# Reordering the mixing stage of a hybrid transformer block: modulation in quadrants, decay tiles on two engines, another order of attention steps

## The chip, the cores and the metric

The program runs on one core of one Trainium2 chip. The metric is the device time of one execution in microseconds. Lower is better. Engines are named as in the profile: PE is TensorE, PEld its weight loads, DVE VectorE, ACT ScalarE, POOL GpSimd, and SP the engine that issues most DMAs. All data is float32.

## What is computed

A first block of the model (512 tokens, width 1024) with four mixers and a mixture of experts, then two layers of a second block. The part that matters here is the first block up to its output projection:

```python
mod = silu(c) @ ada_w + ada_b
sh1, sc1, g1, sh2, sc2, g2 = split(mod, 6)
h = rms_norm(x, norm1_g) * (1 + sc1) + sh1
y = hybrid_mixer(h)
x = x + g1 * y
h = rms_norm(x, norm2_g) * (1 + sc2) + sh2

# hybrid_mixer: proj = h @ w_in, split in columns for
# a: differential attention, 4 heads of 2 maps, keys of 32
# b: block attention (block 256, top 3: all causal keys here), 4 heads of 64
# c: gated linear attention, chunks with decay:
bcum = cumsum(g)
o_inter = (q * exp(bcum)) @ state
att = einsum(q_i, k_j, exp(bcum_i - bcum_j)), causal
o = o_inter + att @ v
state = exp(b_last) * state + (k * exp(b_last - bcum)).T @ v
# d: gated linear recurrence (conv of 4, sigmoid gates, scan, gelu)
```

## The kernel before

The program is a row of stages, each a block in which every engine has its own instruction list. The lists meet at a barrier at the end of each block, and semaphores order them within. The stages concerned are, in order: `project1_stage` (h @ w_in), `mixing_stage`, `attention_stage` under the name "mix", a transpose stage "turn_mix" and the output projection "out1". After them come the second norm, the routing, the experts and the second block.

Weights flow through a ring of three slots of 2 MB, filled by SP in the order of the plan (`load_chunks`). A chunk is loaded into its slot once the matmul group that read the slot's last chunk is done. The mixing stage uses eight chunks of ada_w, and the chunks of w_out follow.

`mixing_stage` does four things at once. Its order is written out by hand, one list per engine.
- **Modulation.** `modulate(i)` on PE multiplies the condition vector, spread over the columns of `cond_rows`, by chunk i of ada_w, so that the result stands in all rows it fills: 512 columns as two halves of 64 rows and 256 columns, for eight blocks of the contraction, and a matmul with `ones` for the bias. `take_mod(i)` on ACT copies each half to both halves of the rows of `k.mod`. That row is used by later stages. There are two banks for it, so `modulate(i)` waits for `take_mod(i - 2)`.
- **Gated linear attention (c).** DVE sums the decays to `b`. For each tile t of 128 tokens, the tensor `ksub[:, t]` holds, for each of 8 reference positions, the keys with their relative decay. It is made in three steps: POOL subtracts the reference and clamps (L1048, 8 instructions of 128x128 a tile, the decay spread), ACT takes the exponential (`raise_tile`), DVE multiplies by the keys (`key_tile`). The queries `qsub` are made by DVE, per head into its own 32 rows (L1403), from the exponential of `ex` (ACT, L1246). Then, for each tile: `att_tile` (PE, 8 matmuls), `mask` (DVE), `outputs` and `update` (PE), `next_state`, `take_out` and `sum_out` (DVE).
- **Gated recurrence (d).** `convolve` (DVE), `lru_gates` (PE), sigmoids and exponentials (ACT), a product `gated` (DVE, L1392) and `lru_tail` (DVE).
- **Head norms of a and b.** `square` (ACT, with `ksub[2]` and `ksub[3]` as room for the squares, which is why the decay spread of tile 2 waits for all four sums), `sum_squares` and `normalize` (DVE), `turn` (PE transposes of q and k into banks) and `take_turned` (ACT for even numbers, DVE for odd ones).

`attention_stage` runs 24 steps. A step is a pair of maps for one tile i of 128 queries: scores against 128(i + 1) keys (L634), transposes of the exponentials (L647), and values (L658). The list of PE is software-pipelined:

```python
for n in range(n_steps):
    if n + 2 < n_steps:
        scores(n + 2)
    if n + 1 < n_steps:
        turn(n + 1)
    values(n)
```

Each pass of that loop is called a round here. Sixteen steps are of differential attention, whose two maps use 32 rows of PE each. Eight are of block attention, with 64 rows each. They stand one kind after the other; within a head i runs 3, 2, 1, 0 or 0, 1, 2, 3. Beside them, `HeadNorm` does one product on the modulation row (DVE, round 0), and the norm of the finished differential heads (square at round 16, sum at 17, root at 22, product at 23).

## Time and profile before

| what | value |
|---|---|
| median of 3 runs | 3010.74 us (3009.67 to 3011.48) |
| the profiled execution's own time | 3006.7 us |
| its span in the trace | 3004.9 us |
| its mean granted clock of PE | 0.952 |
| mixing stage | about 213.6 to 289.6 us |
| attention stage "mix" | about 289.6 to 371.5 us |
| busy over the whole span | PE 92%, DVE 39%, ACT 26%, POOL 11% |

A row of a timeline gives the start in microseconds from the span's start, how long the row lasted, the engine, the line, the operation, what it writes and reads, shapes, how many instructions are merged in it (x) and, in brackets, for how long its engine was idle before it and what ended the wait.
### The profile page before, as it was taken

The page shows a single profiled execution, that of the slowest core. Times are in us where ns is not written, and L with a number is a line of the kernel's source. Part 1 is how long each engine was busy: PE and PEld are TensorE (multiplying, and loading weights), DVE is VectorE, ACT ScalarE, POOL GpSimd, SP SyncE. Part 2 cuts the span into 40 slices and gives each one's busy share as a digit, 9 for nine tenths or more (in the row PEclk, how much of TensorE's full clock was granted, in tenths as well). Part 3 has the DMA queues.
Part 4 walks back from the last instruction along what each step waited for, and adds up shares of the span by engine and source line. Part 5 has one row for each costly group of instructions (what it writes and reads, how often), then busy time and mean ns, then how long its engine had stood idle before and what let it go on. Part 6 is the DMA issues. An engine that isn't in the chain of part 4 may idle for free. (4 is left out here: it accounts for less than half of the span.)

```text
span 3004.9 us, 55460 instructions
## 1 busy us (share of the span) xinstructions
PE 2776.7 (92%) x21321; PEld 1848.2 (62%) x21322; DVE 1180.6 (39%) x2449; ACT 789.6 (26%) x1689; POOL 316.7 (11%) x415
## 2 busy tenths in 40 slices
PE   5998977989998989999978999999999999899997
PEld 4986774333333323333337677788887768788886
DVE  1235644222222222232224575434343566454332
ACT  3225520000000000010104355322232345343221
POOL 1003000222222212222220000000000000000000
PEclk8998886999999989999999999999999999999999
DMA  7244027999999999799964400122232220023220
GB/s 200 78 138 172 1 78 295 401 409 398 402 407 411 399 411 408 292 399 407 409 251 130 139 1 2 56 91 106 84 112 61 83 85 2 30 83 111 85 104 37
DMA packets 181479, 583.68 MB, mean 194 GB/s; under 512 B 31243, under 2 KB 70348, under 8 KB 132108
## 3 DMA queue, kind: packets, MB, share of 16 engines
q1 hardware_dynamic: 160422, 557.17, 47.4%
...
## 5 line engine op out<-in xcount | busy, mean ns | idle before, releaser
L1846 PE MATMUL moe_up<-expert_w,mod 128*32 128x512 f32 x2040 | 244.9, 611 | 28.7 <-issue 19.5
L1957 DVE TENSOR_TENSOR mod<-moe_up,mod 128x512 f32<-128x512 f32 x85 | 58.8, 692 | 480.2 <-PE moe_up L1846 479.2
L1846 PE MATMUL moe_up<-ring,mod 128*32 128x512 f32 x1696 | 209.3, 619 | 22.2 <-DMA ring<-in_exp_w_up 17.3
L303 PE MATMUL mlp_bank<-mlp_hT_hi,mlp_w 128*128 128x512 f32 x512 | 199.7, 390 | 0.0
L304 PE MATMUL mlp_bank<-mlp_hT_lo,mlp_w 128*128 128x512 f32 x512 | 199.5, 390 | 0.0
L305 PE MATMUL mlp_bank<-mlp_hT_hi,mlp_w 128*128 128x512 f32 x512 | 199.5, 390 | 0.0
L304 PE MATMUL mlp_bank<-mlp_w,mlp_u_hi 128*128 128x512 f32 x512 | 199.5, 390 | 0.0
L305 PE MATMUL mlp_bank<-mlp_w,mlp_u_lo 128*128 128x512 f32 x512 | 199.5, 390 | 0.0
L303 PE MATMUL mlp_bank<-mlp_w,mlp_u_hi 128*128 128x512 f32 x512 | 199.5, 390 | 0.0
L1934 ACT ACTIVATE mod<-mod 128x256 f32<-128x256 f32 x85 | 35.4, 417 | 565.7 <-DVE mod L1959 565.7
L347 ACT ACTIVATE mlp_w<-ring 128x1024 fp32r<-128x1024 f32 x128 | 125.1, 1052 | 207.6 <-PE mlp_bank L305 207.6
L1846 PEld LDWEIGHTS moe_up<-expert_w,mod 128*32 128x32 f32 x2040 | 63.2, 112 | 170.5 <-issue 141.0
L356 DVE TENSOR_TENSOR mlp_w<-ring,mlp_w 128x1024 fp32r<-128x1024 f32 x128 | 148.1, 1220 | 6.1 <-ACT mlp_w L347 6.1
L1808 POOL DMA_INDIRECT mixed_rows<-mod,moe_place x86 | 135.8, 1579 | 122.0 <-DVE mod L1974 113.6
L1846 PEld LDWEIGHTS moe_up<-ring,mod 128*32 128x32 f32 x1696 | 51.0, 112 | 136.4 <-issue 91.9
L1863 PE MATMUL moe_down<-expert_w,mod 128*32 128x256 f32 x2176 | 133.0, 381 | 0.0
L1462 DVE TENSOR_TENSOR x<-x,mlp_bank 128x512 f32<-128x512 f32 x64 | 43.9, 687 | 222.2 <-PE mlp_bank L305 222.2
L1930 ACT ACTIVATE mod<-moe_turn_hid 128x256 f32<-128x256 f32 x85 | 32.6, 383 | 341.1 <-PE moe_turn_hid L1854 341.1
L2524 DVE TENSOR_TENSOR mlp_relu<-mlp_relu 128x512 f32<-128x512 f32 x64 | 44.3, 692 | 191.5 <-ACT mlp_u_hi L2521 191.5
L1797 POOL CAST moe_index<-row_token 128x1 uint32 (+1 forms) x87 | 20.1, 232 | 857.3 <-PE moe_turn_rows L1839 613.8
L303 PEld LDWEIGHTS mlp_bank<-mlp_hT_hi,mlp_w 128*128 128x128 f32 x512 | 96.2, 188 | 20.5 <-DVE mlp_hT_lo L510 0.4
L305 PEld LDWEIGHTS mlp_bank<-mlp_w,mlp_u_lo 128*128 128x128 f32 x512 | 96.2, 188 | 20.0
...
## 6 DMA issues: line engine op xcount, KB each, us to landing
...
```

Source lines behind the costliest of these rows:

```text
L303: nc.tensor.matmul(out, lhsT.hi, rhs.hi, start=(i == 0), stop=False)
L304: nc.tensor.matmul(out, lhsT.hi, rhs.lo, start=False, stop=False)
L305: mm = nc.tensor.matmul(out, lhsT.lo, rhs.hi, start=False, stop=last)
L347: nc.scalar.activation(halves.hi[:, at], w[:, at], ACT.Copy).then_inc(hi_made, 1)
L356: nc.vector.tensor_tensor(halves.lo[:, at], w[:, at], halves.hi[:, at].bitcast(F32), ALU.subtract).then_inc(lo_made, 1)
L1462: return nc.vector.tensor_tensor(k.x[:, t, cols], k.x[:, t, cols], psum, ALU.add)
L1808: pool.indirect_dma_start(x_parts, bass.IndirectOffsetOnAxis(ap=place[:], axis=0), y, None, compute_op=op).then_inc(y_stored, 16)
L1846: mm = nc.tensor.matmul(up[quarter[q], :], rowsT[:, c % 2, quarter[c // 2]], w[:, q], start=(c == 0), stop=(c == UPS - 1))
L1863: mm = nc.tensor.matmul(down[quarter[q], 0:YCOLS], hidT[:, h, quarter[at]], w[:, h, q * YCOLS:(q + 1) * YCOLS], start=(at == 0 and h == 0) ...
L1934: nc.scalar.activation(sig, gate, ACT.Sigmoid, scale=ALPHA).then_inc(sig_ready, 1)
L1957: nc.vector.tensor_tensor(pre, up[:], bias_up, ALU.add).then_inc(up_taken, 1)
L2524: chain(nc.vector.tensor_tensor(r, r, r, ALU.mult))
```

## The change

In `mixing_stage`:
- A modulation is computed in four quadrants of 32 rows and 128 columns each. ACT copies it with one instruction into `mod_rows`. In the attention stage SP stores four rows of that tile to DRAM and reads them back with one DMA into all rows of `k.mod`; the load of `norm2_row` moves there too.
- The decay spread of tiles 0 and 2 is on DVE, as two instructions of 128x1024 each; tiles 1 and 3 stay on POOL. The queries are one product on DVE and four copies on POOL. The product `gated` goes from DVE to POOL, as two instructions.
- The lists of PE, ACT and DVE are in another order, and two of the turned copies go from DVE to ACT.

In the attention stage the two kinds of steps alternate (two differential ones, one of the others) for the first 15 steps, and the work beside them is at other rounds: the product on the modulation row at round 19, the head norm at rounds 21 to 23.

```diff
+class MixRest:
...
+    def sync(self, sp):
+        sp.dma_start(self.norm2_row[:], row(self.k.a["norm2_g"][0])).then_inc(self.norm2_loaded, 16)
+        sp.dma_start(self.mod_dram.rearrange("(i q n) -> q i n", q=PARTS, n=COL // PARTS), self.mod_rows[0:P:BR]).then_inc(self.rows_stored, 16)
+        sp.wait_ge(self.rows_stored, 16)
+        sp.dma_start(self.k.mod[:].rearrange("p i n -> p (i n)"), row(self.mod_dram)).then_inc(self.rows_spread, 16)
+        sp.wait_ge(self.rows_spread, 16)
 
     def scalar(self, act, n):
         nc = self.k.nc
         if n == self.made:
             act.wait_ge(self.out_taken, self.made)
             nc.scalar.activation(self.sq[:], self.v, ACT.Square).then_inc(self.squared, 1)
-        if n == self.n_steps - 2:
+        if n == self.made + 1:
             act.wait_ge(self.summed, 1)
             nc.scalar.activation(self.rms[:], self.ss[:], ACT.Sqrt, bias=self.k.eps[:], scale=1.0 / A_DV).then_inc(self.rooted, 1)
 
     def vector(self, dve, n):
         k, nc = self.k, self.k.nc
-        if n == 0:
-            dve.wait_ge(k.norm2_loaded, 16)
+        if n == self.made - 2:
+            dve.wait_ge(self.norm2_loaded, 16)
+            dve.wait_ge(self.rows_spread, 16)
             nc.vector.scalar_tensor_tensor(k.mod[:, 2, :], k.mod[:, 2, :], 1.0, self.norm2_row[:], ALU.add, ALU.mult)
         if n == self.made + 1:
             dve.wait_ge(self.squared, 1)
             nc.vector.tensor_reduce(self.ss[:], self.sq[:], X, ALU.add).then_inc(self.summed, 1)
-        if n == self.n_steps - 1:
+        if n == self.made + 2:
             dve.wait_ge(self.rooted, 1)
             nc.vector.reciprocal(self.inv[:], self.rms[:]).then_inc(self.inverted, 1)
...
-            nc.gpsimd.tensor_copy(cond_rows[:], k.cond[:].unsqueeze(2).to_broadcast([P, ND, half])).then_inc(spread, 1)
-            nc.gpsimd.memset(qsub[:], 0.0).then_inc(zeroed, 1)
-            for t in range(NT):
-                pool.wait_ge(cum, t + 1)
-                if t == 2:
-
-                    pool.wait_ge(summed, len(heads))
+            def spread_tile(t):
                 bt = b[:, tile(t)]
                 for n in range(NSUB):
                     ref = bt[:, n * SUB + SUB // 2:n * SUB + SUB // 2 + 1]
-                    nc.gpsimd.tensor_scalar(ksub[:, t, n, :], bt, ref, -DECAY_CLAMP * C_TAU, ALU.subtract, ALU.max).then_inc(key_spread, 1)
+                    nc.gpsimd.tensor_scalar(ksub[:, t, n, :], bt, ref, -DECAY_CLAMP * C_TAU, ALU.subtract, ALU.max).then_inc(key_spread[1], 1)
+
+            nc.gpsimd.tensor_copy(cond_rows[:], k.cond[:].unsqueeze(2).to_broadcast([P, ND, BR])).then_inc(spread, 1)
+            nc.gpsimd.memset(qsub[:], 0.0).then_inc(zeroed, 1)
+            pool.wait_ge(cum, 2)
+            spread_tile(1)
+            pool.wait_ge(q_scaled, 1)
+            pool.wait_ge(zeroed, 1)
+
+            pool.wait_ge(key_spread[1], NSUB)
+            for h in range(C_HEADS):
+                r = slice(h * C_DK, (h + 1) * C_DK)
+                nc.gpsimd.tensor_copy(qsub[r, :, h, :], ex[r, :].rearrange("p (n s) -> p n s", s=SUB)).then_inc(qsub_made, 1)
+            pool.wait_ge(opened, 4)
+            pool.wait_ge(conv_done, 2)
+            pool.wait_ge(qsub_made, C_HEADS)
+            for j in range(2):
+                nc.gpsimd.tensor_tensor(xc[:, j, :], xc[:, j, :], gates[:, 1, j, :], ALU.mult).then_inc(gated, 1)
+            pool.wait_ge(cum, NT)
+
+            pool.wait_ge(summed, len(heads))
+            spread_tile(3)
...
-                    for h in range(2):
-                        nc.tensor.matmul(to[half * h:half * h + half, 0:width], cond_rows[:, j, :], w[:, j, width * h:width * h + width],
+                    for q in range(PARTS):
+                        nc.tensor.matmul(to[BR * q:BR * q + BR, 0:width], cond_rows[:, j, :], w[:, j, width * q:width * q + width],
                                          start=(j == 0), stop=False)
-                for h in range(2):
-                    mm = nc.tensor.matmul(to[half * h:half * h + half, 0:width], k.ones[0:1, 0:half],
-                                          k.mod[0:1, part, c + width * h:c + width * (h + 1)], start=False, stop=True)
+                for q in range(PARTS):
+                    mm = nc.tensor.matmul(to[BR * q:BR * q + BR, 0:width], k.ones[0:1, 0:BR],
+                                          k.mod[0:1, part, c + width * q:c + width * (q + 1)], start=False, stop=True)
                 mm.then_inc(k.groups_done, 1)
...
-            modulate(2)
-            modulate(3)
+            for i in range(2, 6):
+                modulate(i)
...
             def take_mod(i):
-                n = chunks[i]
-                part, c = (n - FIRST_MOD) * COL // D, n * COL % D
                 act.wait_ge(k.groups_done, first_group + i + 1)
-                for h in range(2):
-                    src = mod_bank[i % 2][half * h:half * h + half, 0:width]
-                    for to in range(2):
-                        copy = nc.scalar.activation(k.mod[half * to:half * to + half, part, c + width * h:c + width * (h + 1)], src, ACT.Copy)
-                copy.then_inc(mod_taken, 1)
+                nc.scalar.activation(mod_rows[:, i, :], mod_bank[i % 2][:, 0:width], ACT.Copy).then_inc(mod_taken, 1)
...
-            nc.scalar.activation(silu, silu, ACT.Silu).then_inc(silu_made, 1)
-            nc.scalar.activation(dxg[:, 2:4, :], dxg[:, 2:4, :], ACT.Gelu_apprx_tanh).then_inc(gelu_made, 1)
...
+            nc.scalar.activation(silu, silu, ACT.Silu).then_inc(silu_made, 1)
             square_out(0)
+            nc.scalar.activation(dxg[:, 2:4, :], dxg[:, 2:4, :], ACT.Gelu_apprx_tanh).then_inc(gelu_made, 1)
...
+            def spread_tile(t):
+                bt = b[:, tile(t)]
+                ref = bt.rearrange("p (n s) -> p n s", s=SUB)[:, :, SUB // 2:SUB // 2 + 1].to_broadcast([P, NSUB, P])
+                chain(nc.vector.tensor_tensor(ksub[:, t], bt.unsqueeze(1).to_broadcast([P, NSUB, P]), ref, ALU.subtract))
+                nc.vector.tensor_scalar(ksub[:, t], ksub[:, t], -DECAY_CLAMP * C_TAU, None, ALU.max).then_inc(key_spread[0], 1)
...
+            spread_tile(0)
...
+            nc.vector.tensor_tensor(ex[:], fm[:, 0, :], ex[:], ALU.mult).then_inc(q_scaled, 1)
...
-            nc.vector.tensor_tensor(xc[:], xc[:], gates[:, 1], ALU.mult).then_inc(gated, 1)
...
-            for h in range(C_HEADS):
-                r = slice(h * C_DK, (h + 1) * C_DK)
-                nc.vector.tensor_tensor(qsub[r, :, h, :], fm[r, 0, :].rearrange("p (n s) -> p n s", s=SUB),
-                                        ex[r, :].rearrange("p (n s) -> p n s", s=SUB), ALU.mult).then_inc(qsub_made, 1)
...
-            take_turned(1)
-            sum_out(3)
             take_turned(3)
...
-            take_turned(5)
             take_turned(7)
...
-            attention_stage(k, "mix", [diff_step(h, i) for h in range(A_HEADS) for i in tiles(h)]
-                            + [moba_step(g, i) for g in range(2) for i in tiles(g)], beside=lambda ctx, sems: HeadNorm(k, tok, norm2_row, ctx, *sems))
+            diffs = [diff_step(h, i) for h in range(A_HEADS) for i in tiles(h)]
+            mobas = [moba_step(g, i) for g in range(2) for i in tiles(g)]
+            steps = []
+            for n in range(5):
+                steps += [diffs[2 * n], mobas[n], diffs[2 * n + 1]]
+            steps += diffs[10:] + mobas[5:]
+            attention_stage(k, "mix", steps, beside=lambda ctx, out_taken: MixRest(k, tok, mod_rows, mod_dram, ctx, out_taken, 5 * 3 + 6))
```

What the table of orders looks like at three places. First ACT, from the end of its logarithms to the exponential of `ex` and the queries' and keys' decays behind it (`mod<-mixing_bank` and `mod_rows<-mixing_bank` are the modulation's copies, `mixing_ksub<-tok` the squares of the head norm, `mixing_ksub<-mixing_ksub` a decay tile). Before:

```order
L1203 ACTIVATE mixing_ksub<-tok 128x1024 x2
L1196 ACTIVATE mod<-mixing_bank 64x256 x4
L1238 ACT_TABLE_LOAD
L1238 ACTIVATE qk<-mixing_bank,lru_b 128x512 x2
L1203 ACTIVATE mixing_ksub<-tok 128x1024
L1238 ACTIVATE qk<-mixing_bank,lru_b 128x512 x2
L1203 ACTIVATE mixing_ksub<-tok 128x1024
L1196 ACTIVATE mod<-mixing_bank 64x256 x4
L1243 ACTIVATE qk<-qk 128x512 x2
L1196 ACTIVATE mod<-mixing_bank 64x256 x4
L1246 ACT_TABLE_LOAD
L1246 ACTIVATE mixing_ex<-mixing_ex 128x512
```

and with the change:

```order
L1213 ACTIVATE mod_rows<-mixing_bank 128x128
L1219 ACTIVATE mixing_ksub<-tok 128x1024 x2
L1253 ACT_TABLE_LOAD
L1253 ACTIVATE qk<-mixing_bank,lru_b 128x512 x2
L1213 ACTIVATE mod_rows<-mixing_bank 128x128
L1253 ACTIVATE qk<-mixing_bank,lru_b 128x512 x2
L1213 ACTIVATE mod_rows<-mixing_bank 128x128
L1257 ACTIVATE qk<-qk 128x512 x2
L1259 ACT_TABLE_LOAD
L1259 ACTIVATE mixing_ex<-mixing_ex 128x512
```

Two squares have left this stretch and stand behind the exponential, and each modulation's copy is one instruction. The silu and gelu activations, which opened the list, are gone from ahead of it.

Second PE, from the modulation ahead of the first attention tile to the second tile of the gated linear attention (L1098, later L1124, is the turn of the keys). Before:

```order
L1062 MATMUL mixing_bank<-ring,mixing_cond_rows 64x256 x16
L1065 MATMUL mixing_bank<-mod,ones 64x256 x2
L1098 MATMUL mixing_bank<-ident,mixing_kout 128x128
L1088 MATMUL mixing_bank<-mixing_qsub,mixing_ksub 128x64 x8
L1062 MATMUL mixing_bank<-ring,mixing_cond_rows 64x256 x16
L1065 MATMUL mixing_bank<-mod,ones 64x256 x2
L1088 MATMUL mixing_bank<-mixing_qsub,mixing_ksub 128x64 x8
```

and with the change:

```order
L1088 MATMUL mixing_bank<-ring,mixing_cond_rows 32x128 x32
L1091 MATMUL mixing_bank<-mod,ones 32x128 x4
L1124 MATMUL mixing_bank<-ident,mixing_kout 128x128
L1114 MATMUL mixing_bank<-mixing_qsub,mixing_ksub 128x64 x8
L1088 MATMUL mixing_bank<-ring,mixing_cond_rows 32x128 x32
L1091 MATMUL mixing_bank<-mod,ones 32x128 x4
L1114 MATMUL mixing_bank<-mixing_qsub,mixing_ksub 128x64 x8
```

Ahead of the first of these rows stand five modulations where there were three. One follows between the tiles as before, and one stands ahead of the last tile; before, one stood there, one ahead of the last outputs and one among the turns.

Third POOL, its whole list in the mixing stage. Before:

```order
L1038 COPY mixing_cond_rows<-cond 128x512
L1039 MEMSET mixing_qsub 128x2048
L1048 ISA
L1048 TENSOR_SCALAR mixing_ksub<-mixing_b 128x128 x32
```

and with the change:

```order
L1055 COPY mixing_cond_rows<-cond 128x256
L1056 MEMSET mixing_qsub 128x2048
L1053 ISA
L1053 TENSOR_SCALAR mixing_ksub<-mixing_b 128x128 x8
L1065 COPY mixing_qsub<-mixing_ex 32x32x16 x4
L1070 TENSOR_TENSOR qk<-qk 128x512 x2
L1053 TENSOR_SCALAR mixing_ksub<-mixing_b 128x128 x8
```

POOL spreads two tiles instead of four, and between them it places the queries and does the product for the recurrence.

## Rows read from the trace of the kernel before

**Rows 1.** windows: us, PE, PEld, DVE, ACT, POOL busy; PEclk; DMA share, GB/s

```profile
213.60:289.60 76.00, 66.78 (x491) 45.11 (x491) 50.78 (x82) 46.95 (x86) 30.38 (x34) 0.84 0.61 214
289.60:371.50 81.90, 78.52 (x504) 61.27 (x504) 49.50 (x132) 40.26 (x124) 0.00 (x0) 0.79 0.01 2
291.50:325.60 34.10, 33.62 (x148) 25.49 (x145) 17.39 (x44) 13.53 (x44) 0.00 (x0) 0.50 0.00 1
240.00:245.00 5.00, 1.42 (x7) 1.42 (x8) 4.91 (x7) 4.96 (x12) 5.00 (x5) 0.53 1.04 385
```

**Rows 2.** timeline of ACT, mixing stage: start, length, instruction, [idle before]

```profile
213.70 1.28 ACT L1221 ACT_TABLE_LOAD   x1 [0.27 <-PEq L256]
...
217.37 1.06 ACT L1222 ACTIVATE dxg<-dxg 128x1024 f32<-128x1024 f32 x1
...
235.02 1.55 ACT L1196 ACTIVATE mod<-mixing_bank 64x256 f32<-64x256 f32 x4
...
237.88 0.63 ACT L1246 ACTIVATE mixing_ex<-mixing_ex 128x512 f32<-128x512 f32 x1
```

**Rows 3.** timeline of DVE, mixing stage

```profile
229.01 0.54 DVE L1387 TENSOR_SCALAR qk<-qk,mixing_lru_lam 128x512 f32<-128x512 f32 x1
...
232.76 1.21 DVE L1392 TENSOR_TENSOR qk<-qk 128x1024 f32<-128x1024 f32 x1
...
238.60 3.01 DVE L1403 TENSOR_TENSOR mixing_qsub<-fm,mixing_ex 32x512 f32<-32x512 f32 x4 [3.24 <-ACT mixing_ex L1246]
...
275.04 0.68 DVE L1314 TENSOR_TENSOR mixing_att<-mixing_bank,upper_incl 128x512 f32<-128x512 f32 x1
...
287.94 1.40 DVE L1357 TENSOR_SCALAR qk<-mixing_bank,gain_cols 128x512 f32<-128x512 f32 x2
```

**Rows 4.** groups of POOL: instruction, count | busy us, mean ns | idle before

```profile
L1048 POOL TENSOR_SCALAR mixing_ksub<-mixing_b 128x128 f32<-128x128 f32 x32 | 28.0, 891 | 8.6 <-DVE mixing_b L1374 8.6
...
L2067 POOL TENSOR_TENSOR tok<-tok,cos_a 128x512 f32<-128x512 f32 x2 | 4.3, 2156 | 0.2
...
L1038 POOL COPY mixing_cond_rows<-cond 128x512 f32<-128x512 f32 x1 | 0.6, 610 | 201.4 <-POOLq L256 201.4
```

**Rows 5.** timeline of PE, mixing stage

```profile
243.58 0.48 PE L1098 MATMUL mixing_bank<-ident,mixing_kout 128*128 128x128 f32 x1 [5.36 <-DVE mixing_kout L1407]
243.85 3.52 PE L1088 MATMUL mixing_bank<-mixing_qsub,mixing_ksub 128*128 128x64 f32 x16
...
270.34 2.00 PE L1088 MATMUL mixing_bank<-mixing_qsub,mixing_ksub 128*128 128x64 f32 x16
...
273.60 0.32 PE L1131 MATMUL mixing_bank<-tok,mixing_kt 128*32 128x64 f32 x8
273.85 3.67 PE L1062 MATMUL mixing_bank<-ring,mixing_cond_rows 128*64 128x256 f32 x32
```

**Rows 6.** page, part 5: a group of the expert stage

```profile
L1863 PE MATMUL moe_down<-expert_w,mod 128*32 128x256 f32 x2176 | 133.0, 381 | 0.0
```

**Rows 7.** timeline of PE, attention stage

```profile
289.90 1.13 PE L634 MATMUL mix_s<-qk 32*128 32x512 f32 x4 [1.83 <-PEq L974]
...
295.27 1.22 PE L634 MATMUL mix_s<-qk 32*128 32x256 f32 x4
...
322.35 1.92 PE L647 MATMUL mix_t<-ident,mix_p 128*128 128x128 f32 x8
...
326.18 0.92 PE L634 MATMUL mix_s<-qk 32*128 32x384 f32 x4
...
329.86 0.70 PE L634 MATMUL mix_s<-qk 32*128 32x256 f32 x4
...
346.92 0.92 PE L634 MATMUL mix_s<-qk 64*128 64x384 f32 x4
```

**Rows 8.** timeline of PE in norm_rows_stage, later in the program

```profile
440.63 1.58 PE L577 MATMUL norm_bank<-ident,h 128*128 128x128 f32 x8 [0.36 <-DVE h L556]
```

**Rows 9.** window of that place, columns as in rows 1

```profile
441.00:443.00 2.00, 1.24 (x9) 1.01 (x7) 2.00 (x3) 0.00 (x0) 0.00 (x0) 0.83 0.68 264
```

133 lines of the change are left out of this document (69 added, 64 removed).

## The prediction

> **What bounds the kernel now.** I read the windows first. The change touches two stages that run one after the other behind barriers: mixing_stage, 213.6 to 289.6 us, and the attention stage, 289.6 to 371.5 us [rows 1]. What comes later (expert stage, second block) starts when they end, so a microsecond saved here is one saved at the end. In the mixing stage PE is busy 66.8 of 76.0 us, yet no single engine is the bound: the chain of waits moves between them. The timelines show it. ACT is busy without a gap from 213.7 to the exponential at 237.88 [rows 2]; DVE makes the masked queries from it, 238.60 to 241.6 [rows 3]; PE has waited 5.36 us when it goes on at 243.58 [rows 5], now at 1.2 GHz. Then PE is the path, its modulation among the attention tiles, up to 275; from the last mask at 275.04 DVE works without a gap to 289.34 [rows 3]. In the attention stage PE is busy 78.5 of 81.9 us [rows 1], and 34.1 us of it lie at PEclk 0.50, the lower of its two levels.
>
> **The mixing stage, part by part.**
> *ACT's opening.* The silu and gelu activations leave the front: 213.70 to 218.43 with two table loads, 4.7 us [rows 2]. They come back behind the last decay tile with the same two loads. Three modulation copies stand ahead of the exponential; each was four instructions in 1.55 us [rows 2] and becomes one of 128x128. By the rate of those, 0.38 us for 256 columns, I take 0.28, so 3.8 us less. Two squares of 1.05 us go behind it. That is 10.6 us of work less, but ACT now runs into waits (gate matmul 1.2 us, third modulation 1.5 us, others 1.1): the exponential ends near 231.7, not 238.51. DVE, which adds one spread tile here (a subtraction of 1.21 us and a clamp of twice 0.54 [rows 3], 2.4 us in all), is ready by then.
> *Queries.* DVE's four products take 3.01 us [rows 3]. Now one product (0.7) and four POOL copies follow. The trace has no 32x512 POOL copy: the nearest is 0.61 us for 128x512, the far bound is a POOL product of 2.16 us [rows 4]. I take 0.61: queries ready at 235.1, at worst 241.3.
> *PE up to the first tile.* Modulations 0 to 5 now all stand ahead of it. One costs 3.67 us plus 0.58 for the bias at full clock [rows 5]. In quadrants it is 72 matmuls of 128 columns instead of 36 of 256. The short quadrant matmuls of 64 columns start 31 ns apart (eight in the 0.25 us from 273.60 to 273.85 [rows 5]); those of 256 columns in the expert stage 61 ns apart (133.0 us over 2176 [rows 6]). 128 columns lie between; I take 33 ns, as the columns add little to the first: 2.4 us each, 3.9 us at 1.2 GHz. The weights limit it now: 2.1 MB at 385 GB/s [rows 1] are 5.4 us a chunk, and a slot frees when its modulation ends (the first three near 219, 223.5 and 228). The third chunk is in near 220, the next three follow near 226, 231 and 237. So modulation 5 starts at 236.8, the clock having fallen in the gap before it, and ends at 240.8; the first tile starts at 241.1 against 243.85. The POOL copies, even at mid-range, are hidden behind this wait.
> *PE from there to the last mask.* Before, 31.2 us (243.85 to 275.04). Now, at full clock: tile 2.0 [rows 5], modulation 2.4, tile 2.0, outputs 1.0, update and key turn 0.6, tile 2.0, outputs 1.7, update and turn 0.6, modulation 2.4, tile 2.0, outputs 1.4, update 0.3, state and hand-off 0.5: 18.9. The last mask is at 260.0. The decay tiles must keep up: tile 2 is spread by DVE by 241.8, tile 3 by POOL after its copies and two gating products of 2.16 us [rows 4], 239.4 to 246.4 at 0.89 us each for eight. ACT then raises it, runs silu, and DVE has tile 3 ready at 253.1, 2.6 us before PE asks.
> *DVE's tail.* 14.3 us before. Two of its four turned copies go to ACT (2 x 0.7 [rows 3]), one sum goes ahead, one product comes in: 13.5. The end is at 273.5 against 289.34: 15.8 us less. I take 15, as a dozen hand-offs are rounded down. Bounds: matmuls at 61 ns delay every modulation by 2.0 us and eat 8 to 9 us; a clock at 1.2 GHz through the tiles costs 3; POOL copies at 2.16 us cost up to 5, by the third decay tile. DVE or POOL faster than taken gives 2 back. So 7 to 18.
> *The DMAs.* norm2_row (0.5 MB) leaves the mixing stage's queue; in the attention stage SP issues it, a 16 KB store, waits, and a 2 MB spread. At 385 GB/s they need about 7 us plus two landings; DVE asks for them at step 19 of 24, some 45 us on. Hidden. Nothing is queued on SP behind them.
>
> **The attention stage.** The matmuls are the same, in another order. The price of the clock is in the trace: seven rounds at 1.2 GHz took 30.9 us (295.27 to 326.18), the seven of the same shapes at 2.4 GHz 17.1 us (329.86 to 346.92) [rows 7]. The question is when the clock rises. Before, it fell 1.6 us into the stage after a gap of 1.8 us, and came back only at 325.6, in a stretch that holds eight transposes and the values after them (from 322.35 [rows 7]). The opening before had a 384-column and a 256-column score step on 32 rows, with eight and six transposes. Now the second step is a 64-row one of 512 columns, its two matmuls filling all rows of the array, and eight transposes, 384 columns, and eight transposes follow. That is denser than anything in the first 30 us before. I expect the rise 5 to 8 us in, so nearly all of 13.8 us is saved. Against it: the first scores now run at 1.2 GHz, since PE stands half idle before the stage (+1.1); the product on the modulation row, 1.22 us on DVE, moves from a slack round into one where DVE has little room (+1.2). The head norm now ends in the last three rounds; its square, sum and root fit beside values still running, at most +1. Sum: 11 us less. Bounds: 13.8 less if all goes at full clock, 0 if it rises as late as before.
> Do transposes count for the clock? In norm_rows_stage PE does nothing but transposes, and the granted clock rises within them, 0.83 over 441 to 443 us [rows 8, 9]. The Trainium skill ("TensorE: Matmul & The Clock Gate", Part 4) says that full clock does not engage for transposes; by that rule the rise would hang on scores and values alone, and the sum would be 15 instead of 26. The trace disagrees with it.
>
> **Rivals.**
> 1. The clock rises late: the opening is too thin, small steps follow, and only the two long steps 11 and 12 lift it, three rounds later than before. For it: 34 us at 0.50 before [rows 1]. Mixing keeps 15, attention gives 0 to -3: 2996. The skill's rule on transposes would give this one.
> 2. The quadrant matmuls start no faster than about 61 ns apart: modulation costs 4.4 us as before, mixing gains 7, attention 11: 2993. For it, rows 6; against it, the 31 ns. The skill (same page, Part 2, step 2) names about 62 ns per matmul where the sequencer decodes in microcode; that is this rival, and the 31 ns speak against it here.
> 3. Slower: the mixed order keeps the attention stage at 1.2 GHz to its end. A round costs 2.0 us more there (13.8 over 7). The 15 of mixing are used up once the clock stays low for eight rounds beyond the seven of before; with all 23 rounds it is 16 x 2.0 - 15 = 17 slower: 3028. Against it: steps of both long kinds come early.
> 4. The change doesn't shorten mixing because POOL's work (copies, gating, third decay tile) is twice what I take; tile 3 is late by 5 to 7 us: 2990.
>
> **The numbers.** Sum: -15 and -11, 26 us. The profiled execution took 3006.7 us (span 3004.9), 4 us under the median of 3010.7; against the median the forecast is 2985, for the profile a span near 2979. Chances: both gains 0.55, rival 1 0.2, rival 2 0.1, rival 4 0.08, rival 3 0.03, several of these together 0.04. The range, from both gains at their upper ends (18 and 13) to rival 1 with a poorer mixing stage (10 and 0): 2979 to 3000. A measurement tells about 0.2%, 6 us, from no change. Faster by more 0.93, within 0.03, slower 0.04.
>
> **What would show it.** Right: exponential of ex ending near 232, first tile near 241, mixing stage about 60 us long, attention stage about 70 with PEclk 1.00 from its tenth microsecond. Wrong: modulation over 3 us at full clock; PE waiting for chunks past 240; tile 3's clamp on POOL past 248; PEclk 0.50 past 290.

## The result, and the profile after

The changed kernel took 2980.97 us (median of four runs, 2976.33 to 2988.59), the kernel before 3010.49 us beside it (four runs, 3009.67 to 3011.48). The ratio is 0.9894, with a 95% interval of 0.9858 to 0.9930; times 3010.49 that is 2978.6 us. The forecast was 2985 in a range of 2979 to 3000, so the median lies just inside the lower end and the time by the ratio 0.4 us below it; the interval is 2968 to 2989 us, far wider than that distance. Something else stands out: the kernel before spread over 1.8 us, the changed one over 12.3. The profiled execution is the slowest of its four runs (span 2986.8, own time 2988.59).

Windows of the changed kernel, columns as in [rows 1]: the mixing stage, the attention stage, and within it the stretch at the lower clock.

```profile
214.15:274.32 60.17, 48.10 (x780) 38.75 (x780) 50.66 (x80) 38.16 (x65) 25.15 (x24) 0.83 0.74 263
274.32:351.17 76.85, 73.36 (x504) 56.90 (x505) 49.12 (x132) 40.22 (x125) 0.00 (x0) 0.87 0.10 35
276.30:296.80 20.50, 20.03 (x88) 15.78 (x87) 8.17 (x17) 8.00 (x24) 0.00 (x0) 0.50 0.30 115
```

From first matmul to first matmul, mixing went from 76.2 us (213.74 to 289.90) to 60.2, attention from 81.7 (to 371.58) to 76.9. What follows took 2.3 us longer than before, beginning at once: the transposes behind attention ran at full clock before (2.81 us at 371.58) and here fall into a stretch at 1.2 GHz (4.48 us). With a start 0.4 us later the sum is -18.1, the difference of the spans. The 2.3 us are not all the change's: what follows attention took 2633.3, 2637.7 and 2636.7 us in the three profiles of the kernel before, and 2635.6, 2639.9 and 2635.6 in those of the changed one.

PE in the changed kernel: the mixing stage, for [rows 5], and the first transposes behind the attention stage:

```profile
215.96 1.95 PE L1088 MATMUL mixing_bank<-ring,mixing_cond_rows 128*32 128x128 f32 x64
...
233.43 3.64 PE L1088 MATMUL mixing_bank<-ring,mixing_cond_rows 128*32 128x128 f32 x64 [3.38 <-DMA ring<-in_ada_w]
...
238.80 3.58 PE L1088 MATMUL mixing_bank<-ring,mixing_cond_rows 128*32 128x128 f32 x64 [1.14 <-DMA ring<-in_ada_w]
...
242.83 1.90 PE L1114 MATMUL mixing_bank<-mixing_qsub,mixing_ksub 128*128 128x64 f32 x16
...
351.17 4.48 PE L403 MATMUL turn_mix_bank<-ident,tok 128*128 128x128 f32 x24 [2.12 <-PEq L596]
```

ACT, for [rows 2]: the exponential of the decay differences, and that of the fourth decay tile, which waits for POOL.

```profile
230.42 0.63 ACT L1259 ACTIVATE mixing_ex<-mixing_ex 128x512 f32<-128x512 f32 x1
...
247.77 1.06 ACT L1223 ACTIVATE mixing_ksub<-mixing_ksub 128x1024 f32<-128x1024 f32 x1 [2.63 <-POOL mixing_ksub L1053]
```

POOL (in [rows 4] it only spread tiles and the conditions): the second tile, the four query copies, the two gating products, the fourth tile.

```profile
223.94 7.73 POOL L1053 TENSOR_SCALAR mixing_ksub<-mixing_b 128x128 f32<-128x128 f32 x8 [7.65 <-DVE mixing_b L1398]
231.93 4.19 POOL L1065 COPY mixing_qsub<-mixing_ex 32x512 f32<-32x512 f32 x4 [0.26 <-DVE mixing_ex L1414]
236.30 3.48 POOL L1070 TENSOR_TENSOR qk<-qk 128x512 f32<-128x512 f32 x2 [0.18 <-POOL mixing_qsub L1065]
239.95 7.79 POOL L1053 TENSOR_SCALAR mixing_ksub<-mixing_b 128x128 f32<-128x128 f32 x8 [0.17 <-DVE mixing_ss L1318]
```

DVE, for [rows 3]: the last mask and the last turned copy.

```profile
260.20 0.68 DVE L1339 TENSOR_TENSOR mixing_att<-mixing_bank,upper_incl 128x512 f32<-128x512 f32 x1
...
273.24 0.75 DVE L1384 TENSOR_SCALAR qk<-mixing_bank,gain_cols 128x512 f32<-128x512 f32 x1 [0.40 <-PE mixing_bank L1173]
```

The four runs carry a hint about the spread. Their spans and mean granted clocks give the time at 1.2 GHz (a mean of 0.954 over 2986.8 us is 275 us at half clock): 275 us in the slowest, 244 in the fastest (2974.5, 0.959). So 31 us of lower clock go with 12.3 us of time. The clock is given to three digits, and one unit of the last is 6 us at 1.2 GHz, so this is a rough figure.

### The profile page after: what moved, and what is told of

Read it like the earlier page. It is cut to its first block and busy times, and to the rows that moved or that the text cites. A ratio compares the mean times of both kernels' runs of the same rounds, so it can differ in the third digit from the quotient of the medians.

```text
span 2986.8 us, 56010 instructions
## 1 busy us (share of the span) xinstructions
PE 2756.0 (92%) x21609; PEld 1838.9 (62%) x21610; DVE 1180.0 (40%) x2447; ACT 781.1 (26%) x1667; POOL 312.8 (10%) x405
## 5 line engine op out<-in xcount | busy, mean ns | idle before, releaser
L303 PEld LDWEIGHTS mlp_bank<-mlp_w,mlp_u_hi 128*128 128x128 f32 x512 | 96.2, 188 | 19.9
## 6 DMA issues: line engine op xcount, KB each, us to landing
expert_w<-in_exp_w_up SPq DMA_DIRECT2D x97, 1024.0 KB, 10.8
hT<-in_exp_w_up SPq DMA_DIRECT2D x24, 1024.0 KB, 10.8
```

The source lines that it names most:

```text
L303: nc.tensor.matmul(out, lhsT.hi, rhs.hi, start=(i == 0), stop=False)
```

## The experiments

There were eighteen experiments, on four chips; five of them ran a kernel that had run before, unedited. "Stage" is from first matmul to first matmul, "low" the time at 1.2 GHz within it, in each one's profile. Times of different chips are not compared where it can be helped; the experiments told in one section did not all run on the same chip. The kernel before took part each time: over these four chips it has 89 runs.

### Is it one kernel or several? The changed kernel and the one before, again

> The changed kernel again, unedited, to see whether its runs differ among themselves by the same amount and by the same cause. The four runs known so far lie 12.3 us apart (2976.33 to 2988.59) where those of the kernel before lie 1.8 us apart, and the slowest of them spent about 275 us at the lower clock (span 2986.8, mean granted clock 0.954) against 244 us in the fastest (2974.5, 0.959): 31 us of lower clock for 12.3 us of time. Theory (the clock in the attention stage rises sooner in some runs and later in others): times between 2975 and 2989, the profiled run's attention stage 66 to 75 us long, and the time of a run grows by about 0.4 us with each us at 1.2 GHz. Rival (the spread comes from DMAs or from elsewhere in the span): mean granted clock the same in every run while the times differ, attention 74.7 us again. Rival (an accident of the chip it ran on): runs within 2 us of each other.

> The kernel before once more, unedited, with a profile. On the chips used since the first comparison its runs fall into two groups, 3009 to 3015 us at a mean granted clock of 0.950 and 3027 to 3033 us at 0.944, nothing between; the profile known is of the first group. 18 us for about 44 us more at 1.2 GHz. Theory (the second group keeps 1.2 GHz through a stretch of one of its two stages, as the changed mixing stage did in one profile): if the profiled run is of the second group, its mixing stage is near 90 us instead of 76.2, or its attention stage near 98 instead of 81.7, and the rest within 3 us of the first profile. Rival (the whole span is a little slower): stages longer in proportion, by 0.6%. If the profile is of the first group again, stages within 1 us of the first profile, and nothing is told of the second.

> The kernel before, one more profile, for the group of runs at 3027 to 3033 us. The attention stage in the old order was seen at 1.2 GHz for 34 us in two profiles of the kernel before and for 72 us in a profile of the changed mixing stage with the old order, where it took 102.4 us instead of 81.1 and the clock rose only when the first 64-row steps came. Theory: if this run is of the slow group its attention stage is 98 to 103 us long at 1.2 GHz for some 70 us, mixing 76 us. Rival: mixing 90 us or more with attention 81.7. If it is of the first group it shows the first profile's stages again and nothing more.

The changed kernel again: 2983.8 us (six runs, 2982.7 to 2992.0), ratio 0.9883 (0.9850 to 0.9916). This profile caught the other way in which its attention stage goes:

```profile
213.20:273.00 59.80, 46.03 (x780) 37.41 (x780) 50.67 (x80) 38.05 (x65) 24.91 (x24) 0.89 0.75 265
273.00:341.90 68.90, 65.53 (x505) 50.43 (x506) 48.98 (x132) 40.33 (x125) 0.00 (x0) 0.98 0.10 40
274.90:278.30 3.40, 3.06 (x14) 1.70 (x10) 1.93 (x2) 2.12 (x6) 0.00 (x0) 0.50 0.60 188
```

Mixing is the same to 0.4 us. Attention is 8.0 us shorter, with 17 us less at 1.2 GHz, on the same instructions. The spread is there again (9 us, up to 2992.0, a little over the 2989 expected), so the rival of an accident falls, and the two profiles show that the clock in attention is part of it. It is not all of it. The span is only 5.0 us shorter (2981.8 against 2986.8), as what follows attention took 4.3 us longer in this profile. Over the sixteen runs of the unedited changed kernel, time grows by 0.29 us per us of lower clock, with a correlation of 0.77.

The kernel before does the same on a larger scale. Of its 89 runs 48 lie between 3007 and 3018 us (median 3011.4, the lower group) and 41 between 3025 and 3033 (3029.6, the upper group), with none between; the four of the first comparison were all of the lower group, which with 48 to 41 is an accident of four draws. Over the 23 runs on the first of these chips, time grows by 0.43 us per us of lower clock. The second profile was of the lower group and repeated the first (stages 76.0 and 81.7). The third, at 3029.4 us, was of the upper one:

```profile
214.70:291.80 77.10, 67.70 (x493) 45.68 (x493) 50.78 (x82) 46.99 (x87) 30.36 (x34) 0.85 0.61 212
291.80:390.80 99.00, 95.52 (x504) 74.95 (x504) 50.01 (x132) 40.06 (x124) 0.00 (x0) 0.64 0.00 1
293.80:365.50 71.70, 70.86 (x313) 55.65 (x312) 33.76 (x92) 25.42 (x84) 0.00 (x0) 0.50 0.00 1
```

From first matmul to first matmul attention is 99.1 us, 17.4 longer than the 81.7 of the first profile, and mixing 0.9 us; that is the group. PE was busy for 70.9 of the 71.7 us at 1.2 GHz. The clock came back in the first round with a 64-row score step (PE, same profile):

```profile
360.33 2.08 PE L634 MATMUL mix_s<-qk 64*128 64x512 f32 x4
362.34 0.39 PE L636 MATMUL mix_s<-causal_half,ident_half 128*128 128x128 bf16 x2
362.53 1.91 PE L647 MATMUL mix_t<-ident,mix_p 128*128 128x128 f32 x8
364.24 2.01 PE L658 MATMUL mix_o<-tok,mix_pt 128*128 128x64 f32 x12
366.18 0.92 PE L634 MATMUL mix_s<-qk 64*128 64x384 f32 x4
```

In the lower group it came back without any 64-row step. The first line is from the first profile of the kernel before, where the clock rose at 325.6; the second is the same round in this profile, where it did not:

```profile
320.15 2.08 PE L634 MATMUL mix_s<-qk 32*128 32x512 f32 x4
```
```profile
322.04 2.08 PE L634 MATMUL mix_s<-qk 32*128 32x512 f32 x4
```

What the two places share is that a round with 512-column scores follows another one. The scores of the first pair start at 314.94 and 320.15 in the first profile and at 316.82 and 322.04 in this one; those of the next pair, whose second step is the first with 64 rows, at 355.12 and 360.33 in this one. So the number of rows alone does not explain when the clock rises.

### The two halves of the change, each alone

The new mixing stage with the old attention order (diff), and the old mixing stage with the new order (the same lines the other way round in the kernel before, its `made` at 21):

```diff
-            steps = []
-            for n in range(5):
-                steps += [diffs[2 * n], mobas[n], diffs[2 * n + 1]]
-            steps += diffs[10:] + mobas[5:]
-            attention_stage(k, "mix", steps, beside=lambda ctx, out_taken: MixRest(k, tok, mod_rows, mod_dram, ctx, out_taken, 5 * 3 + 6))
+            steps = diffs + mobas
+            attention_stage(k, "mix", steps, beside=lambda ctx, out_taken: MixRest(k, tok, mod_rows, mod_dram, ctx, out_taken, 16))
```

> The changed kernel with the attention steps in the order of before (all sixteen differential steps, then the eight others), the squares of the head norm made at step 16: only the mixing stage and the place of the small DMAs are new. Theory (the two gains are separate, some 15.5 us in mixing and the rest in the order of the steps): 3010.5 - 15.5 = 2995 us, within 2993 to 2998, the mixing stage 59.9 us long as in the changed kernel, the attention stage near 80 us again with the clock at 1.2 GHz for some 30 us of it. Rival A (the order of the steps is worth nothing, the shorter mixing stage only moves the attention stage to another moment of the clock): 2976 to 2989 as the changed kernel. Rival B (part of mixing's gain is paid back because attention begins with a colder TensorE): 3000 or more.

> The kernel before with nothing but the new order of the attention steps (differential, other, differential, five times over; head norm moved to match). Theory (the order brings the clock's rise forward, because steps with 64 rows stand among those with 32): attention stage 64 to 75 us instead of 79.6, so 3010.5 less 5 to 15, most likely 2997 us. Rival A (the order is worth nothing by itself): 3009 to 3012. Rival B (the norm at the end of the stage lies open and takes it back): attention's matmuls end 5 to 15 us earlier, but the next stage starts with a gap of 1 us or more that it had not before, 3000 or more.

New mixing alone: 3004.1 us (twelve runs), ratio 0.9950 (0.9924 to 0.9976), and again two groups, six runs at 2995.5 to 2998.9 and six at 3009.3 to 3018.4. The lower one, 2997.8, is 15 us under the lower group of before on that chip (3012.9): the forecast's 15, if the same way of attention is compared, which no profile of those six shows. The median itself lies outside the 2993 to 2998 expected and where rival B put it (3000 or more), but not for rival B's cause, as attention took 81.1 us. New order alone: 3000.1 us (twelve runs), ratio 0.9939 (0.9917 to 0.9961), ten runs at 2997 to 3002 and two at 3012; nothing is left at 3030. Rival B's 3000 is touched, but not its gap: PE waited 2.12 us ahead of the next stage, as before. Its attention stage took 68.7 us against 81.7, behind an unchanged mixing stage of 76.0:

```profile
289.80:358.50 68.70, 65.69 (x504) 50.30 (x505) 48.98 (x132) 40.40 (x125) 0.00 (x0) 0.98 0.01 2
```

Its ten are 13 us under the same group. So, lower group against lower group, the two gains are separate and add up to 28, where the whole change has 29 on that chip (2983.8). By plain medians, with both groups in each, they are 10.8 and 14.8, and the whole change 31.1. Rival A of either experiment falls. The first one's profile, though, is at 3010.5 us for a cause of its own, mixing:

```profile
213.68:287.60 73.92, 63.31 (x779) 51.68 (x780) 50.50 (x80) 38.26 (x65) 24.20 (x24) 0.65 0.61 214
240.20:284.60 44.40, 40.73 (x335) 35.55 (x324) 22.98 (x42) 16.03 (x26) 6.43 (x8) 0.50 0.41 140
287.60:368.70 81.10, 77.44 (x505) 60.36 (x505) 49.40 (x132) 41.38 (x126) 0.00 (x0) 0.81 0.09 34
```

The very code that took 59.8 and 60.2 us in the changed kernel took 73.9 here, since the clock fell at 240.2, 1.2 us after the second wait for weights (1.58 us, up to 239.05), and stayed down through all four decay tiles. Where the same code took 59.8 us it fell at 237.3 and for 3.4 us only.

### What inside the mixing stage made the gain: three parts undone

Chunks in halves again (the quadrants' DMA kept), the third tile on POOL again, silu and gelu in front again:

```diff
-                    for q in range(PARTS):
-                        nc.tensor.matmul(to[BR * q:BR * q + BR, 0:width], cond_rows[:, j, :], w[:, j, width * q:width * q + width],
+                    for q in range(0, PARTS, 2):
+                        nc.tensor.matmul(to[BR * q:BR * q + 2 * BR, 0:2 * width], cond_rows[:, j, :], w[:, j, width * q:width * q + 2 * width],
```
```diff
@@ gpsimd @@
+            spread_tile(2)
             spread_tile(3)
@@ vector @@
-            spread_tile(2)
```
```diff
@@ scalar @@
+            nc.scalar.activation(silu, silu, ACT.Silu).then_inc(silu_made, 1)
+            nc.scalar.activation(dxg[:, 2:4, :], dxg[:, 2:4, :], ACT.Gelu_apprx_tanh).then_inc(gelu_made, 1)
             act.wait_ge(gate_ready, 1)
```

> The changed kernel with the modulation chunks multiplied in two halves of 64 rows by 256 columns again, taken by four small ACT copies a chunk instead of one; the one DMA that spreads the rows stays, and so does every order. A chunk then costs TensorE 4.3 us at full clock instead of 2.3 (rows of before: 3.67 and 0.65), 2 us more in each of eight, and ACT some 0.8 us more. Theory (between the decay tiles and their outputs TensorE is on the path only in part: chunk 5 stands ahead of the first tile, chunks 6 and 7 among the tiles): mixing stage 3 to 6 us longer than 59.9, total 3 to 6 us above the changed kernel's median in the same rounds. Rival A (TensorE has slack in the whole stage, its waits for VectorE, ScalarE and GpSimd hide it): within 1 us of 59.9. Rival B (every chunk lies on the path): 16 us more or so.

> The changed kernel with the third decay tile spread by GpSimd again instead of VectorE (GpSimd then does the second, third and fourth, VectorE only the first). Theory (the fourth tile waits for GpSimd; a tile takes it 7.8 us): the fourth tile's exponential starts near 255.5 instead of 247.7 us, the last mask and the end of the stage come 6 to 8 us later, total 6 to 8 us above the changed kernel. Rival A (VectorE is what the tiles wait for; 1.9 us less of its work helps): within 2 us of the changed kernel. Rival B (the stretch gives TensorE a longer idle time and the lower clock with it): 10 us or more above.

> The changed kernel with the silu and the gelu at the head of ScalarE's work in the mixing stage again, as before the change, nothing else moved. They take 7 us or so there. Theory (ScalarE's opening chain sets when the decay can be raised and the query rows be ready, so all that stands in front of it is on the path): the first decay tile 5 to 7 us later than 242.8, of which 1 to 3 us come back because ScalarE has less to do behind, total 4 to 6 us above the changed kernel. Rival A (the weights of chunks 4 and 5 set the first tile, TensorE reaches it at 242.8 only because they land at 233 and 239): first tile at most 2 us later, total within 2 us of the changed kernel. Rival B (all 7 us are on the path): 7 us above.

Halves: stage 66.9 us, +6.8 to +7.1, somewhat over the 3 to 6 expected; 2989.1 us against 2983.8 of the changed kernel on that chip, +5.3, within them. TensorE is on the path, in part of its chunks. Its clock stayed full from the stage's start to 267.7 us, so the price of two us a chunk is not a matter of the clock.

Third tile on POOL: stage 63.8 us, +3.6 to +4.0, not 6 to 8; 2986.8 us, where no unedited changed kernel stood beside it (the filled one there has 2983.6, the changed one elsewhere 2983.8). The direction of the theory holds, its size does not. The sixteen spreading instructions in a row took 745 ns each, where the eights of the changed kernel took 966 and 974; DVE had less work beside them here, but that this is the cause was not tested:

```profile
238.43 11.92 POOL L1053 TENSOR_SCALAR mixing_ksub<-mixing_b 128x128 f32<-128x128 f32 x16 [0.18 <-DVE mixing_ss L1319]
```

Silu and gelu in front: stage 61.9 us, +1.7 to +2.1, and the time is no different, as rival A said: 2982.9 us, between 2977.2 and 2995.9. Two table loads and two activations, 4.7 us, moved the exponential by only 1.9 us (18.8 us into the stage instead of 16.9), because ACT had 2.7 us of waits behind them (1.44, 1.04 and 0.26) that swallowed the rest, and the first decay tile came 2.0 us later (30.7 us into the stage instead of 28.7).

```profile
231.28 0.63 ACT L1261 ACTIVATE mixing_ex<-mixing_ex 128x512 f32<-128x512 f32 x1
```

### What ends last in the new mixing stage: two shortcuts

```diff
-            for i in range(2, 6):
+            for i in range(2, 5):
                 modulate(i)
             turn_keys(0)
             att_tile(0)
-            modulate(6)
+            modulate(5)
```
(chunk 6 then stands ahead of the third tile), and, in the other kernel, the gating product given back to DVE.

> The changed kernel with modulation chunk 5 behind the first decay tile instead of ahead of it, and chunk 6 behind the first state update instead of ahead of the second tile; TensorE's order alone, no work added or removed. Theory (the weights of chunk 5, landed at 238.8 us, and the matmuls on them are what the first tile waited for, not ScalarE's opening: its queries were ready at 236.1 and its keys at 233.6): first tile near 237.7 instead of 242.8 us; of these 5 us 1.5 to 3 reach the end of the stage, since the fourth tile's keys are made at 252.8 to 254.0 whatever TensorE does; stage 57 to 58.5 us, total 1.5 to 3 us less. Rival A (the first tile was bound by GpSimd's and VectorE's work after all): first tile at 241 or later, nothing gained. Rival B (the earlier tiles run on a TensorE that has just idled and is at 1.2 GHz): first tile early but 3.5 us long, nothing gained.

> The changed kernel with the gating product of the recurrent branch on VectorE again as one operation instead of on GpSimd as two of 1.74 us. GpSimd then begins the fourth decay tile 3.5 us earlier, VectorE has some 1.2 us more ahead of its second key tile. Theory (TensorE has no idle time between the first and the fourth tile, 242.7 to 259.6 us, so GpSimd's 3.5 us are not on the path): stage within 1 us of 59.8, total within 1.5 us. Rival A (the fourth tile's spread ends last, as the 2.6 us that its exponential waits for GpSimd suggest): 2 to 3.5 us less. Rival B (VectorE is the bound of the opening): 1 to 2 us more.

The first did what it says and gained nothing of the 1.5 to 3 us expected: the first tile starts 22.1 us into the stage instead of 28.7, the stage takes 60.2 us, the runs 2982.9. The timelines of PE and DVE show why:

```profile
235.61 1.97 PE L1114 MATMUL mixing_bank<-mixing_qsub,mixing_ksub 128*128 128x64 f32 x16 [0.53 <-issue]
...
251.48 0.42 DVE L1366 TENSOR_TENSOR tok<-tok,mixing_bank 128x256 f32<-128x256 f32 x1 [4.33 <-ACT mixing_c_sq L1231]
...
252.09 1.22 DVE L1333 TENSOR_TENSOR mixing_ksub<-mixing_ksub,fm 128x1024 f32<-128x1024 f32 x1
```

DVE stands 4.3 us in front of the outputs' square on ACT; that stands behind silu, silu behind the fourth tile's exponential, and this behind POOL's spread (3.16 us of ACT's idle time). A second chain, POOL to ACT to DVE, is as long as PE's, as far as one profile tells. The gating product moved off POOL did not shorten that one either (60.4 us and 2981.1, as its theory said, though for another reason): POOL then waited 4.1 us for DVE's sums, whose squares lie in the same memory as the tile, and began it no sooner.

```profile
240.62 7.43 POOL L1053 TENSOR_SCALAR mixing_ksub<-mixing_b 128x128 f32<-128x128 f32 x8 [4.13 <-DVE mixing_ss L1314]
```

Both shortcuts together, with the sums drawn ahead, were not tried.

### Can the clock be held up? Added matmuls, and another order of the steps

The added ones multiply the identity by fm into a bank that is overwritten afterwards:

```diff
+            def fill(n, to):
+                for _ in range(n):
+                    nc.tensor.matmul(to[:], k.ident[:], fm[:, 0, :], start=True, stop=True)
```

> The changed kernel with matmuls that compute nothing of the result put into two idle stretches of TensorE in the mixing stage: six of 128x512 ahead of modulation chunk 4 and two ahead of chunk 5, where TensorE waited 3.4 and 1.1 us for the weights. Their output is overwritten. In the profiles so far this stage ran in two ways with the same code: 59.8 us (two profiles, 10.2 us of the stretch around chunks 4 and 5 at 1.2 GHz) and 73.9 us (one profile, 44.4 us in a row at 1.2 GHz), and the kernel with the halves, whose TensorE is busier there, kept 2.4 GHz through that whole stretch. Theory (the idle stretch at the weights lets the clock fall, and whether it comes back by the first decay tile is a matter of moment): with the stretch filled no 1.2 GHz between 228 and 262 us, mixing stage 57 to 59 us, no run with a late stage; times as the changed kernel or up to 4 us below, the spread carried by attention alone. Rival (the clock falls for a cause of its own, whatever TensorE does): low stretches as before, time unchanged or 1 to 2 us above for the added matmuls.

> The kernel with the filled weight waits, and besides six such matmuls ahead of the fifth turn of the mixing stage, where TensorE waits 3.9 us for VectorE's normalized rows, and two behind the last turn, ahead of the attention stage. Theory (an idle TensorE at the end of mixing is what costs the clock of the last turns and, in a part of the runs, of the first 20 us of attention): the last turns take 3.3 us instead of 5.3, the attention stage has at most one short stretch at 1.2 GHz in every run, times within 4 us of each other and 4 to 8 us below the changed kernel's median. Rival A (the clock in attention is set by attention's own matmuls alone): times spread by 8 us or more as before, at most 2 us gained. Rival B (the added matmuls stand in the way of the turns): 1 to 3 us slower than the changed kernel.

> The changed mixing stage with the attention steps in the old order, as in the second experiment, plus the added matmuls in the two waits for the weights. The second experiment had six of twelve runs at 2995.5 to 2998.9 us and six at 3009 to 3018, and its profile, one of the latter, showed the mixing stage at 73.9 us with 44 us in a row at 1.2 GHz. Theory (the fall in the wait for the weights is where that late stage begins): no run over 3003 us; median 2998. Rival (the stage falls into the lower clock elsewhere too): the two groups again, half and half.

Filling the wait for the weights kept the clock up there in its profile and is worth nothing: mixing 59.8 us and not 57 to 59, the time 2983.6 us, attention in its long form (76.9). The same filling with the old order, below, had 3.4 us at 1.2 GHz in that stretch all the same, from 244.9 us.

```profile
228.00:262.00 34.00, 31.67 (x487) 24.37 (x477) 26.30 (x41) 21.95 (x37) 18.39 (x19) 1.00 0.89 316
```

Six more ahead of the fifth turn stood in the way. Each took 1.2 us, since most of them ran at 1.2 GHz; the six at the weights, at 2.4 GHz, took 0.9 each (the second line, from the profile above):

```profile
269.66 7.34 PE L1080 MATMUL mixing_bank<-fm,ident 128*128 128x512 f32 x12
```
```profile
229.43 5.42 PE L1080 MATMUL mixing_bank<-fm,ident 128*128 128x512 f32 x12
```

Mixing 67.4 us, but attention then ran 68.3 us with the clock at 1.00: 2986.6 us, 3.0 more than with the weight waits filled alone. That is rival B's loss with the theory's clock; the runs lie 6.8 us apart, not within 4. Whether the filling is what kept the clock up is not shown: the kernel with the third tile on POOL had 68.3 us too, without it.

With the old order the filled wait did not help (2997.2 us median, twelve runs from 2983.8 to 3023.2, five of them 3012 or more); the rival holds. Its profile shows that the group at the top need not come from mixing at all:

```profile
276.40:378.80 102.40, 98.69 (x504) 76.99 (x505) 49.95 (x132) 41.05 (x126) 0.00 (x0) 0.62 0.07 27
279.10:350.80 71.70, 70.95 (x313) 56.24 (x313) 31.99 (x90) 25.31 (x84) 0.00 (x0) 0.50 0.08 31
```

It is the 71.7 us of the kernel before once more, ending again in the first 64-row round (at 344.92), which is again the second of two rounds with 512 columns. So the order matters: in none of the profiles with the new one did the clock stay down so long. But it does not decide alone. Three of these twelve runs took 2983.8 to 2987.3 us, as little as the changed kernel, with the old order; none of them has a profile. The next kernels put two 64-row steps first, which are long ones too (512 and 384 columns), so that rows and length are not told apart:

```diff
-            for n in range(5):
-                steps += [diffs[2 * n], mobas[n], diffs[2 * n + 1]]
-            steps += diffs[10:] + mobas[5:]
+            d, m = iter(diffs), iter(mobas)
+            for kind in "MMDMDDMDDMDD" + 9 * "D" + "MMM":
+                steps.append(next(m if kind == "M" else d))
```

> The changed kernel with two steps with 64 rows at the head of the attention stage and a third in fourth place (before that, every third step from the second on); the last differential step is still the twenty-first, the last three steps as they were. In eight profiles with the changed order the stage was 68.3 to 68.9 us long in six, with 0 to 3.4 us at 1.2 GHz, and 76.8 us in two, with 20.5 us. Theory (matmuls over 64 rows bring the clock back, and those of the first ten us decide): never more than 7 us at 1.2 GHz in the stage, 69 us or less in every run, so times 0 to 3 us below the changed kernel's 2983.6 with no run 5 us above the others. Rival A (the clock's rise is decided by what TensorE did in the mixing stage's end): the profiled stage may be 76.8 us as well and the runs spread over 8 us as before. Rival B (the first steps now have the longest reductions back to back): 68.9 plus 1 us, no other effect.

> The step order with two 64-row steps first, the six and two added matmuls in the waits for the weights, three ahead of the third turn (where TensorE waits 4 us) and one behind the last; each added matmul took 0.9 us at 2.4 GHz in the earlier runs. Theory (with both stretches filled and the strong steps first no state of the clock is left to chance): mixing 59 to 61 us, attention 68 to 69, times within 4 us of each other and 2980 us or less, the best of all versions. Rival (as with the six matmuls ahead of the fifth turn, which made the stage 7.6 us longer, the added ones stand in the turns' way): 2 to 5 us above the order alone.

> The order with the first decay tile ahead of chunk 5 and the attention order with two 64-row steps first, together. Theory (the gains are separate: 1.5 to 3 us in mixing, 1.5 us and no late rise of the clock in attention): stage of mixing 57 to 58.5 us, attention 67.3, median 2976 to 2980 on a chip where the changed kernel has 2983.8. Rival (mixing's end moves against the clock and gives it back): median 2981 or more.

> The changed kernel, unedited, on the same chip as the next one. Median 2980 to 2985 us; about one run in four 5 to 10 us above the rest, at a lower mean clock, which are those with 20.5 us at 1.2 GHz in attention; the profile shows mixing 59.8 to 60.4 us and attention either 68.9 or 76.8.

> The changed kernel with two 64-row steps at the head of attention, unedited from its first run. Theory (no late rise, and the stage 1.5 us shorter in any case): median 1.5 to 3 us below the changed kernel's on this chip, attention 67.3 us in the profile. Rival (the gain is given back in mixing, which took 63.4 us in its first profile, or the runs spread as much): medians within 1.5 us.

In all four profiles with this order attention took 67.3 us, with at most 0.9 us at 1.2 GHz. Four are few: with the order of the changed kernel 8 of 11 profiles had no late rise either. The last one of the four:

```profile
274.40:341.70 67.30, 63.46 (x505) 49.64 (x505) 48.95 (x132) 40.33 (x125) 0.00 (x0) 1.00 0.11 41
```

Times: 2980.6 us alone (six runs), 2980.8 with added matmuls too, 2980.9 with the first tile drawn forward, each against a kernel before that itself lay in its two groups. All three miss a part of what was expected: the first runs are 10.5 us apart and not 5, the second 6.7 and not 4, and the mixing stage of the third took 62.5 us instead of 57 to 58.5, as its rival has it. Side by side on one chip the changed kernel had 2986.8 us (2981.5 to 2989.2; its profile has the long attention, 76.9) and this order 2981.8 (2976.6 to 2984.6): 5.0 us less, over the 1.5 to 3 expected. The changed kernel's own median was forecast at 2980 to 2985, with one run in four late; three of the six took 2988 or more. Both are clearly faster than the kernel before (ratios 0.9905, 0.9877 to 0.9932, and 0.9890, 0.9864 to 0.9917), but as these intervals overlap, that the order beats the changed kernel is likely rather than shown; what is shown is the stage, 67.3 us four times out of four. Mixing took 63.4 us in one of its profiles and 60.0 in the other, so what spread is left (10.5 and 8.0 us) comes in part from there. This also says that attention's clock was not the whole of the changed kernel's spread. The added matmuls and the earlier tile bring nothing beyond it.

| kernel | median us | mixing | attention (low) |
|---|---|---|---|
| before, lower group / upper group | 3011.4 / 3029.6 | 76.2 / 77.1 | 81.7 (34.1) / 99.1 (71.7) |
| changed, two ways seen | 2981 to 2987 | 59.8 to 60.2 | 68.9 (3.4) or 76.9 (20.5) |
| two 64-row steps first | 2980.6, 2981.8 | 63.4, 60.0 | 67.3 (0 to 0.4) |

## Why the prediction was right or wrong

**Right: the mixing stage as a whole.** Forecast 60 us long, measured 60.2; 15 us less, measured 16.0. Its steps: exponential of ex ending at 231.7, measured 231.05; last mask at 260.0, measured 260.2; DVE's tail 13.5, measured 13.8. The last mask owes its closeness to luck: the first tile came 1.7 us late, and PE from there to the last mask took 17.4 us instead of 18.9. The quadrants were the step with the most at stake: 33 ns a matmul taken, 30 measured (1.95 us over 64), and with halves the stage is 7 us longer, near the 8 us that rival 2 would have cost. Rival 2 falls. The about 62 ns per matmul that the Trainium skill gives for decoding in microcode ("TensorE: Matmul & The Clock Gate", Part 2, step 2) do not show in these 128*32 matmuls.

**Right in the sum, wrong in the piece: ACT's opening.** I counted its 10.6 us of removed work as what brings the exponential forward, and the first tile as bound by the weights. Both are so, but then the first piece is nearly free: 4.7 us of silu and gelu in front cost 1.9 us. The first tile came at 242.8, not 241.1, because the weights of chunk 5 landed at 238.8, 2 us later than my 5.4 us a chunk said; that the matmuls on them would run at 1.2 GHz was in the sum. And even that was not the end of the matter: the tile 6.6 us earlier brings nothing, since POOL's fourth tile, by way of ACT, sets DVE's pace just as late.

**Wrong in size, both ways: POOL.** Its copies took 1.05 us each, not 0.61; queries ready at 236.1 instead of 235.1. Its gating products took 1.74, not 2.16. The two errors all but cancel, and the fourth tile was done at 247.7 instead of 246.4. Rival 4 (twice as slow) did not come.

**The step that failed: the attention stage, -11, bounded by 0 and 13.8.** Two things were wrong in it. The size: when the clock rose as forecast (5.3 us into the stage, I had said 5 to 8), the stage lost 12.8 to 13.0 us, not 11. The three deductions (+1.1 for the first scores, +1.2 for the product on the modulation row, up to +1 for the head norm) amount together to 0.8 to 1.0. The first of them did not come at all: the first scores took 1.13 us, as before, at full clock. With 16.0 instead of 15 from mixing that makes 28.9 instead of 26, and 3010.5 - 28.9 = 2981.6 is close to the measured median of 2981.0. By the ratio the gain is 31.9 us; the 3 us beyond 28.9 lie within its interval and have no term of their own. In the profiled execution, where the clock rose late, attention lost only 4.8 us. The low end of the range, 31 us under the median, left nothing for anything else to vary, and that the result fell next to that end rather than well beyond it is luck too: with runs of the upper group beside it the gain would have been larger. And the form: I gave one time for the clock's rise, with "late" as a rival of a fifth. In truth it differs from run to run in both kernels: in the profiles the old order had between 31 and 79 us of the stage at 1.2 GHz, the new one between 0 and 20.5, and two of the three profiles of the unedited changed kernel had the 20.5, as had three of the eleven with its order of steps. A stage that differs by 8 us for the same instructions made a good part of the 12 us of spread, and a range should have been given for it. The profile alone did not show this; that the profiled execution stood 4 us under the median was no warning either.

**Something like rival 3, the attention stage long at 1.2 GHz, exists, but in the kernel before.** I gave it 3 in 100 for the changed kernel, and for all 23 rounds. The old order shows 71.7 us in a row, to the fifteenth round, eight rounds more than in the lower group. That costs 17.4 us, and my price of 2.0 us a round gives 16. It showed in no profile with the new order. So what the change is worth depends on the group: 27.6 us against the lower one (3011.4 less 2983.8, the median of sixteen runs of the changed kernel), 45.8 against the upper, where the first comparison, with the lower one alone, says 29.5.

**When the clock rises.** Rival 1 had the clock lifted by the two long steps, one behind the other. In the old order that fits the long stretch of all five profiles: it ended in the second of two rounds with 512 columns, in three of them at the first such pair (32 rows), in two at the second (64 rows in its second step). In the new order it fits less well: the two long steps stand at the head, and where the clock rose late, at 296.8, it rose in the round of a 64-row step of 384 columns. Neither length nor rows fit all of it, and no run changed one without the other. Transposes made up a good part of every round. The Trainium skill states that full clock does not engage for transposes (same page, Part 4); the 71.7 us at 1.2 GHz on a busy PE fit that, but the clock also rose in rounds with just as many transposes. The stretch of nothing but transposes in which the clock rose [rows 8, 9] speaks against it, and so do the transposes behind the attention stage of the changed kernel (351.17, 24 of them in 4.48 us): 1.2 GHz from 351.4 to 354.8 us, then 2.4 while they still ran.
